# Even mixer of a two-layer trunk: attention steps in pairs, four modulation panels multiplied by TensorE, the output projection cut in halves

## What is computed

```python
c_act = jax.nn.silu(c)
for l in range(DEPTH):
    mod = (c_act @ ada_w[l] + ada_b[l]).reshape(bsz, 6, 1, D_MODEL)
    sh1, sc1, g1, sh2, sc2, g2 = (mod[:, i] for i in range(6))
    h = rms_norm(x, norm1_g[l]) * (1.0 + sc1) + sh1
    ...
    x = x + g1 * y
    h = rms_norm(x, norm2_g[l]) * (1.0 + sc2) + sh2
    x = x + g2 * grouped_moe(h, router_w, router_b, moe_w_gu[l], moe_w_down[l])

def even_mixer(...):
    u, v, q, k, vd = split_cols(h @ w_in, (SGU_WIDTH, SGU_WIDTH, DIFF_QK, DIFF_QK, DIFF_V))
    a_out = spatial_gating(jax.nn.gelu(u), jax.nn.gelu(v), ln_g, ln_b, w_s, b_s)
    b_out = differential_attention(q, k, vd, lam, subln_g, lam_init)
    return jnp.concatenate([a_out, b_out], axis=-1) @ w_out
```

## Time and profile before

| | us |
|---|---|
| times of three runs | 945.0, 945.79, 954.57 |
| median | 945.79 |
| the profiled execution | 948.7 |
| its span in the trace | 947.0 |
| PE busy | 830.0 (88%) |
| DVE busy | 350.0 (37%) |
| ACT busy | 158.3 (17%) |
| mean granted PE clock | 0.947 |
| read from HBM | 292.18 MB, 310 GB/s over the span |

### The profile page before, as it was taken

The page is one execution under the profiler, slowest core; times in us unless marked ns, Lnnn a source line. Parts: engine busy times, 40 slices in busy tenths (PEclk is TensorE's granted clock), DMA queues, the critical chain, the costliest instruction groups (busy, mean ns, idle before and its releaser), DMA issues.

```text
span 947.0 us, 10346 instructions
## 1 busy us (share of the span) xinstructions
PE 830.0 (88%) x4138; PEld 442.1 (47%) x4138; DVE 350.0 (37%) x845; ACT 158.3 (17%) x386; POOL 23.5 (2%) x65
## 2 busy tenths in 40 slices
PE   5999779889998998866999998999899998998863
PEld 2566554454333332222868887865364333332211
DVE  1186586572111111102888663425274111111102
ACT  2031130132111010001101323322222111010001
POOL 2000000010000000000000000000010000000000
PEclk9999799779999999979999998997979999999989
DMA  9999845599999999999989224240429999999993
GB/s 350 389 339 387 317 176 179 206 371 363 362 410 409 409 409 410 409 409 391 387 295 354 89 90 178 90 178 1 178 94 403 378 407 409 410 409 410 409 410 147
DMA packets 96086, 293.98 MB, mean 310 GB/s; under 512 B 2464, under 2 KB 3104, under 8 KB 96032
## 3 DMA queue, kind: packets, MB, share of 16 engines
q1 hardware_dynamic: 95328, 290.61, 79.9%
q10 hardware_dynamic: 560, 2.10, 0.6%
q0 software_dynamic: 144, 0.52, 0.1%
HBM read 292.18 MB, written 1.05 MB: 310 GB/s over the span
## 4 chain that ended last, share of the span: by engine, by line
PE 47%; issue 26%; SPq 12%; DVE 8%; DMA 3%; ACT 3%; POOL 0%; DVEq 0%; POOLq 0%; ACTq 0%
PE bank L764 15%; SPq L474 12%; PE bank L760 9%; PE bank L986 4%; DMA ring<-w_down_dram 2%; PE bank L1005 2%; DVE gb L1415 2%; PE bank L660 2%; PE bank L822 2%; PE bank L677 1%; PE bank L972 1%; PE bank L633 1%; PE bank L668 1%; PE bank L1020 1%; PE bank L799 1%
## 5 line engine op out<-in xcount | busy, mean ns | idle before, releaser
L986 PE MATMUL bank<-ring,scr 128*64 128x512 f32 (+1 forms) x1088 | 210.5, 624 | 38.4 <-DMA ring<-w_gu_dram 24.8
L764 PE MATMUL bank<-hT,ring 128*128 128x256 f32 x640 | 145.5, 388 | 0.8 <-DVE hT L1477 0.8
L986 PEld LDWEIGHTS bank<-ring,scr 128*64 128x64 f32 (+1 forms) x1088 | 61.2, 131 | 173.4 <-issue 136.6
L764 PEld LDWEIGHTS bank<-hT,ring 128*128 128x128 f32 x640 | 123.8, 195 | 19.3 <-issue 2.0
L1005 PE MATMUL bank<-ring,scr 128*64 128x512 f32 (+1 forms) x544 | 102.2, 597 | 8.9 <-DMA ring<-w_down_dram 8.4
L1903 DVE TENSOR_TENSOR hT<-bank,gb 128x512 f32<-128x512 f32 x28 | 19.4, 692 | 199.8 <-PE bank L1005 199.8
L1415 DVE SCALAR_TENSOR_TENSOR gb<-ring,small,gb 128x512 f32<-128x512 f32 x98 | 73.7, 752 | 3.5
L1005 PEld LDWEIGHTS bank<-ring,scr 128*64 128x64 f32 (+1 forms) x544 | 30.1, 127 | 66.6 <-issue 60.9
L760 PE MATMUL bank<-ring,xh 128*128 128x512 f32 x128 | 58.1, 611 | 1.4 <-ACT xh L1170 1.4
L760 PE MATMUL bank<-ring,hT 128*128 128x512 f32 x128 | 58.2, 611 | 0.7 <-ACT hT L1197 0.6
L1020 PE MATMUL bank<-hT,scr 64*128 64x512 f32 x224 | 55.6, 615 | 1.8 <-DVE hT L1903 1.8
(11 more groups left out here) (238 smaller groups left out, 700.1 us busy)
## 6 DMA issues: line engine op xcount, KB each, us to landing
ring<-w_gu_dram SPq DMA_DIRECT2D x64, 2048.0 KB, 22.3
ring<-w_down_dram SPq DMA_DIRECT2D x32, 2048.0 KB, 23.5
ring<-ada_w_dram SPq DMA_DIRECT2D x24, 2048.0 KB, 14.6
ring<-od_w_in_dram SPq DMA_DIRECT2D x9, 2048.0 KB, 16.0
ring<-ev_w_in_dram SPq DMA_DIRECT2D x5, 2048.0 KB, 19.4
ring<-ev_w_out_dram SPq DMA_DIRECT2D x2, 2048.0 KB, 15.3
ring<-od_w_out_dram SPq DMA_DIRECT2D x2, 2048.0 KB, 8.3
xs<-x_dram ACTq DMA_DIRECT2D x1, 1024.0 KB, 5.8
```

Source lines behind the costliest of these rows:

```text
L764: ins = pe.matmul(banks[h][:, m * 256:(m + 1) * 256], w[:, c, (2 * h + m) * P:(2 * h + m + 1) * P], x_part[:, c, :], start=(c == 0 and m = ...
L986: ins = pe.matmul(b[o:o + r, :].rearrange("p (u f) -> p u f", u=2), h[:, c, r * i:r * i + r], wm, start=(first and c == 0), stop=(last and ...
```

## The change

`ATT_PE` and `ATT_ACT` of layer 0 take the steps in pairs. Panels 8 to 11 are multiplied on PE (`late_rows`), copied out by ACT (`late_row_out`) and summed on PE two at a time (`late_sums`); panels 6, 7, 10 and 11 have their sums in the other pair of buffers. In the load order, ada 8 to 11 stand ahead of the output panels and u moves back by two. ACT, not DVE, empties k and vd. The spatial gating and fill 9 (u's second half) move between attention steps 3 and 4. Fill 10, which multiplies u's half of the output panel 0, comes ahead of the transposes of attention's half. `gate_row2` moves ahead of fill 13.

```diff
 PRE = [[("ada", 0), ("ada", 2), ("in", "v"), ("in", "q"), ("ada", 1), ("ada", 3), ("ada", 4), ("ada", 5), ("in", "k"),
-        ("in", "vd"), ("ada", 6), ("ada", 7), ("in", "u"), ("ada", 8), ("ada", 9), ("out", 0), ("out", 1),
-        ("ada", 10), ("ada", 11)],
+        ("in", "vd"), ("ada", 6), ("ada", 7), ("ada", 8), ("ada", 9), ("in", "u"), ("ada", 10), ("ada", 11),
+        ("out", 0), ("out", 1)],
...
-ATT_PE = ["S0 S1 F T0 S2 A0 T1 S3 A1 F T2 S4 A2 T3 S5 A3 F T4 A4 T5 A5 F".split(),
+ATT_PE = ["S0 S1 F T0 S2 T1 S3 A0 A1 F T2 S4 T3 S5 A2 A3 F T4 T5 A4 A5 F".split(),
...
-ATT_ACT = ["S0 S1 F T0 S2 T1 S3 F T2 S4 T3 S5 F T4 T5 F".split(),
+ATT_ACT = ["S0 S1 F T0 T1 S2 S3 F T2 T3 S4 S5 F T4 F T5 F".split(),
...
+        def acc_of(j):
+            return (acc_even if j // 2 % 2 == 0 else acc_odd)[j % 2]
...
-        DVE_EMPTIES = [{"k", "vd", 0, 1}, {"a", 0, 1}]
+        DVE_EMPTIES = [{0, 1}, {"a", 0, 1}]
...
@@ tensor, even() @@
+                def late_rows(*js):
+                    for j in js:
+                        row_products(bank[j % 2], pre_place(0, ("ada", j)))
+                def late_sums(*js):
+                    take(misc)
+                    pe.wait_ge(late_out, js[-1] - 7)
+                    for j in js:
+                        for m in range(4):
+                            o = 4 * (j % 2) + m
+                            ins = pe.matmul(bank[7][:, o:o + 1], acc_of(j)[:, m * P:(m + 1) * P], thirty_second,
+                                            start=True, stop=True)
+                    give(misc, ins)
...
-                attention(0, 0, [[lambda: (fill(0, 6), fill(0, 7), ada(6), ada(7))],
-                                 [lambda: fill(0, 8)], [lambda: fill(0, 9)]])
-                pe.wait_ge(score_out, 6)
-                pe.wait_ge(vn_ready, 2)
+                attention(0, 0, [[lambda: (ada(6), fill(0, 6), fill(0, 7), ada(7))],
+                                 [lambda: (late_rows(8, 9), fill(0, 8), late_sums(8, 9))],
+                                 [lambda: late_rows(10, 11), spatial, lambda: fill(0, 9)]])
                 for t in range(T):
-                    for g in range(4):
-                        ins = pe.matmul(bank[4 + t][:, g * P:(g + 1) * P], wT[:, g, :], vn[:, t, g * P:(g + 1) * P],
-                                        start=True, stop=True)
-                    ins.then_inc(sgu_mixed, 1)
-                ada(8)
-                for feats, made in ((uu, aout_ready), (vg, bout_ready)):
-                    for t in range(T):
-                        pe.wait_ge(made, t + 1)
-                        transposes([feats[:, t, c * P:(c + 1) * P] for c in range(4)])
-                        if t == 0:
-                            gate_rows(0, 0, (0,) if feats is uu else (1,))
+                    turned(uu, aout_ready, t)
+                late_sums(10, 11)
                 pe.wait_ge(turn_free, turn.n)
                 fill(0, 10)
+                for t in range(T):
+                    turned(vg, bout_ready, t)
+                gate_rows(0, 0)
+                pe.wait_ge(turn_free, turn.n)
                 fill(0, 11)
-                ada(9)
                 fill(0, 12)
-                ada(10)
+                gate_row2(0)
                 fill(0, 13)
-                ada(11)
-                gate_row2(0)
...
@@ scalar, even() @@
+                def values_out():
+                    for h in range(2):
+                        wait_fill(act, 0, 6 + h)
+                        act.activation(vv[:, h, :], fill_bank(6 + h, 0)[:, :], ACT.Copy).then_inc(fill_act[0], 1)
+                def late_row_out(j):
+                    pl = pre_place(0, ("ada", j))
+                    act.wait_ge(panel_done[pl.slot], pl.done)
+                    act.activation(acc_of(j), bank[j % 2][:, :], ACT.Copy).then_inc(late_out, 1)
+                def gelu_table():
+                    act.activation(sm(895, 1), ones[:, 0:1], ACT.Gelu_apprx_tanh)
...
+                attention(0, 0, [[values_out], [lambda: late_row_out(8), lambda: late_row_out(9)],
+                                 [lambda: late_row_out(10), lambda: late_row_out(11), gelu_table],
+                                 [lambda: u_out(0)], [lambda: u_out(1)]])
...
@@ vector, norm(ph) @@
-                if ph == 1:
-                    gate_row2_out()
...
@@ vector @@
+            def late_ada_out(j):
+                misc_in()
+                bias = col[:, C_ADAB:C_ADAB + 96].rearrange("p (l k) -> p l k", l=2)
+                dve.tensor_tensor(mod[:, 0, 4 * j:4 * j + 8], bank[7][:, 0:8], bias[:, 0, 4 * j:4 * j + 8], ALU.add)\
+                   .then_inc(misc_free, 1)
...
@@ vector, even() @@
-                for h in range(2):
-                    wait_fill(dve, 0, 4 + h)
-                    dve.tensor_copy(kT[0][:, 2 * h:2 * h + 2, :], fill_bank(4 + h, 0)[:, :].rearrange("p (c n) -> p c n", c=2))\
-                       .then_inc(fill_dve[0], 1)
+                ada(6)
                 ada_out(0, 4)
                 ada_out(0, 5)
                 dve.wait_ge(dist_done, 2)
                 scores(0, 0, 0, sc, nm_ev[:, 0, :], 0)
                 scores(0, 1, 1, sc, nm_ev[:, 0, :], 0)
                 combine(0, 0)
-                ada(6)
+                combine(1, 1)
+                ada_out(0, 6)
                 ada(7)
-                for h in range(2):
-                    wait_fill(dve, 0, 6 + h)
-                    dve.tensor_copy(vv[:, h, :], fill_bank(6 + h, 0)[:, :]).then_inc(fill_dve[0], 1)
-                ada_out(0, 6)
                 ada_out(0, 7)
-                for j in range(2, 6):
-                    scores(0, j, j, sc, nm_ev[:, 1, :], 0)
-                    combine(j - 1, j - 1)
-                    if j == 3:
-                        sub_norm(0)
-                    if j == 4:
-                        sub_norm_scale(0)
-                        ada(8)
+                scores(0, 2, 2, sc, nm_ev[:, 1, :], 0)
+                scores(0, 3, 3, sc, nm_ev[:, 1, :], 0)
+                sub_norm(0)
+                combine(2, 2)
+                combine(3, 3)
+                late_ada_out(8)
+                scores(0, 4, 4, sc, nm_ev[:, 1, :], 0)
+                scores(0, 5, 5, sc, nm_ev[:, 1, :], 0)
+                combine(4, 4)
                 combine(5, 5)
-                sub_norm(1)
-                ada_out(0, 8)
+                sub_norm_scale(0)
...
-                gates_out(0, (0,))
+                dve.wait_ge(bout_ready, 1)
+                sub_norm(1)
+                late_ada_out(10)
                 sub_norm_scale(1)
-                gates_out(0, (1,))
-                ada(9)
+                gates_out(0)
                 residual(0, 10, 0)
-                ada(10)
                 residual(0, 10, 1)
-                ada_out(0, 9)
-                ada(11)
+                gate_row2_out()
                 residual(0, 10, 2)
-                ada_out(0, 10)
                 residual(0, 10, 3)
-                ada_out(0, 11)
```

More of the change, by code:

```diff
@@ L667, in ada_sum @@
                 for m in range(4):
-                    ins = pe.matmul(bank[7][:, m:m + 1], acc[a][:, m * P:(m + 1) * P], ones[:, 0:1],
+                    ins = pe.matmul(bank[7][:, m:m + 1], acc[:, m * P:(m + 1) * P], ones[:, 0:1],
                                     start=True, stop=True)
@@ L834, in even, with spatial, turned @@
                 base = 0
-                ada = lambda j: ada_sum(acc_even, j % 2, pre_place(0, ("ada", j)))
+                ada = lambda j: ada_sum(acc_of(j), pre_place(0, ("ada", j)))
+                def late_rows(*js):
[10 more added lines that the diff above has]
+                    give(misc, ins)
+                def spatial():
+                    pe.wait_ge(score_out, 6)
+                    pe.wait_ge(vn_ready, 2)
+                    for t in range(T):
+                        for g in range(4):
+                            ins = pe.matmul(bank[4 + t][:, g * P:(g + 1) * P], wT[:, g, :], vn[:, t, g * P:(g + 1) * P],
+                                            start=True, stop=True)
+                        ins.then_inc(sgu_mixed, 1)
+                def turned(feats, made, t):
+                    pe.wait_ge(made, t + 1)
+                    transposes([feats[:, t, c * P:(c + 1) * P] for c in range(4)])
                 fill(0, 0)
@@ L881, in odd @@
                         j = 3 + f if f < 4 else 7
-                        ada_sum(acc_odd, j % 2, pre_place(1, ("ada", j)))
+                        ada_sum(acc_odd[j % 2], pre_place(1, ("ada", j)))
                 pe.wait_ge(*emptied(1, 9))
@@ L909, in conv_rows @@
                     give(misc, ins)
-                ada = lambda j: (lambda: ada_sum(acc_odd, j % 2, pre_place(1, ("ada", j))))
+                ada = lambda j: (lambda: ada_sum(acc_odd[j % 2], pre_place(1, ("ada", j))))
                 attention(1, 0, [[F(10)], [F(11)], [F(12)], [F(13)]])
@@ L1250, in even, with u_out @@
```

(21 more changed lines are left out.)

20 lines of the change are left out of this document (11 added, 9 removed).

## The result

The changed kernel takes 939.86 us (median of 16 runs, 932.27 to 942.4), the kernel before 949.56 in runs beside them (16, 945.0 to 956.55). The ratio is 0.9895, 95% interval 0.9873 to 0.9917. The forecast was 935.8 us against 945.8, a ratio of 0.9894. So the step down is the one predicted, and the absolute figure is 4 us off because the median of the kernel before was itself 3.8 us higher over 16 runs than over the three shown. The profiled execution took 938.6 us, 10.1 less than that of before.

The account below looks back on a forecast made before the run. It took the chain of PE, DVE and ACT before `order` as the bound, with PE setting the mixer. Gains of 6.5 + 5.2 = 11.7 us, less 1.7, left 10.0: 945.8 to 935.8 us, range 933.5 to 938 (chance 0.5).

Parts of the forecast that it names:

- The sum on PE: Mixer of layer 0 from 81.67 us: gapless PE pieces add to 87.5 us, fill 13 ends at 169.2, 6.5 us gained.
- The tail: After fill 13: the transposes start 6.0 us after it and not 11.3, with `gate_row2` done earlier; 5.2 us gained.
- One stretch at the lower clock, 1.7 us, on fill 10: Mixer, after short transposes and one-column matmuls ahead of fill 10: 1.7 us taken off the 11.7 us gain.
- Up to 81.67 nothing moves.: Front of the kernel, until fill 6 starts: the change shifts nothing there, 0 us gained or lost.
- DVE is free at about 78.7 in both: Before fill 6: ada 6's first block fills DVE until the sums of 4 and 5, where DVE was free before too.
- `late_rows`, 1.9 for a panel: New PE work in the mixer: four panels at 1.9 us in a row, 7.6 us; tiling-mode switches priced at 0.
- (c): Mixer: PE's added rows are not hidden, a panel costs 6.9 us; 8.3 us slower, 954 us; chance 0.05.
- The stream ends at about 114: Mixer's weight loads: 19 panels at 5.4 us each, the last landing at about 114 us.
- Nothing waits: Mixer's weight loads in the new order: every panel lands before it is asked for, smallest room 12 us.
- (a): Mixer: two or three more lower-clock stretches of 1.7 us leave 5 to 8 us gained, 938 to 941; chance 0.25.
- (b): Experts' stage: the weight stream takes up the gain, the shorter chain only waits; 943.5 to 947 us; chance 0.07.
- (d): Router and first experts: PE keeps its clock, no slow stretch on fill 10; 12.5 to 15 us gained; chance 0.13.

Follow-up runs that it names:

- load_old: Changed kernel with the old load order: u ahead of ada 8 and 9, output panels ahead of ada 10 and 11; 940.73 us, 0.9898 of the kernel before.
- unpaired: Changed kernel with the attention steps in the old order on PE, ACT and DVE, all else as changed; 946.79 us, 0.9966 of the kernel before.
- row2_last: Changed kernel with `gate_row2` behind fill 13 again and its copy by DVE behind the residuals; 938.61 us, 0.9869 of the kernel before.
- dve_all: Changed kernel with panels 8 to 11 multiplied by DVE in its idle stretches, PE keeping only the sums; 929.6 us, 0.9788 of the kernel before; again 932.42, 0.9825.
- split6: Changed kernel with DVE's panel 6 in two parts around the outs of panels 4 and 5, PE's sum between fills 6 and 7; 938.01 us, ratio 0.9851.
- best2: dve_all with split6 and row2_last, DVE's panels one place later and their sums moved; 929.35 us, 0.9825 of the kernel before.

## Why the prediction was right, point by point

By the profiled executions the transposes of the norm came 10.6 us earlier, where 10.0 was forecast, and four small errors made the 0.6: PE's row starts 0.8 earlier than booked (80.90, not 81.67) and is 0.9 shorter at the upper clock, it has 1.0 more of lower clock (2.7, not 1.7), and the tail is 0.1 longer. The mechanism, a gapless row on PE whose pieces add up, is the one that was forecast; that the figure is so near is partly luck.

- **The sum on PE.** Its first term, the sum of panel 6 ahead of fill 6, starts at 80.90 and fill 13 ends at 170.2: 89.3 us, less 2.7 of lower clock (1.9 on fills 6 and 7, 0.8 on the sum) 86.6, where 87.5 was booked. In load_old, whose row has no piece at the lower clock, it is 86.7 by the rows (80.61 to the end of fill 13 at 167.29). The 0.9 booked too much lies in the four panels of rows (7.1 from start to start, 7.6 booked) and the groups T S T S A A (3.2 each, 3.4 booked). Adding up the pieces by their start-to-start times works where an engine has no gaps. That the pieces would have no gaps was the assumption that carried it, and unpaired shows it is the pairs that make it true (2.83 and 2.44 us of wait without them).
- **The tail.** 6.1 us from fill 13 to the transposes, 6.0 booked. But its reason was half wrong. I credited the 5.2 us to `gate_row2` being gone and the rows at the upper clock; row2_last has `gate_row2` back in the tail and 6.2 us all the same. What made the tail short is that its PE pieces run at the upper clock (L722 1.58, before 2.88; L683 3.64, before 5.17) and that PE comes to them without delay. In the kernel before the sum of panel 11 with the waits about it took the tail's first 3.3 us, from the end of fill 13 at 175.7 to 179.00 (timeline before):

```profile
177.42 1.25 PE L668 MATMUL bank<-ones,gb 128*128 128x1 f32 x8 [1.71 <-DVE mod L1424]
```

With these 3.3 us gone and 2.8 saved by the clock, PE is ahead of the scaled tokens and waits for them, 2.52 us in the kernel after and 1.07 in row2_last. The move costs 1.6 us in front of fill 13 and gives nothing behind it.
- **One stretch at the lower clock, 1.7 us, on fill 10.** One came in the mixer of the profiled execution, but elsewhere and twice as long: 3.5 us from 78 to 86, of which 0.8 lie ahead of the row that the forecast adds up and 2.7 in it. Fill 10 took 7.11. In both executions of dve_all it did fall on fill 10, 8.81. Only the count was right; the rows of one execution before the change could not give the place.
- **"Up to 81.67 nothing moves."** The step that was wrong, though the total hides it. "DVE is free at about 78.7 in both" held for DVE's work but not for its order: the outs of panels 4 and 5 stand behind the whole of panel 6 in its queue, and PE waits 2.45 us. The profiled execution hides this, since its front happened to run 3.2 us earlier (the sum after fill 5 at 74.01, before at 77.21). The 3.2 lie in three pieces: in the kernel before the first transposes (at 11.65) took 3.65 us, the row product behind them 3.12 and fill 0 8.83, in the kernel after 3.34, 1.92 and 7.13.
- **Which part of the front counts.** The 1.5 us of the first two pieces moved DVE as well. The 1.7 of fill 0 did not, and the wait ate it: from the copy behind the second row product (L666 at 20.57, L660 at 22.08 before) to the second sum (77.41, before 78.89) it is 56.8 us in both kernels, and in all eight executions of changed kernels with this order on DVE, whether fill 0 took 7.13 or 8.65. So with a front like that of the kernel before nothing does move, and with fill 0 at the upper clock the kernel before would gain where the changed one waits. Two estimates follow from these rows. With the slow front in both, the second sum stands at 78.9, fill 6 3.6 us later as in load_old, and the transposes 91.95 behind it, at 174.5: 12.5 us gained. With the fast front in both, the kernel before would be 3.2 earlier (its DVE idles 4.74 us before k's copies, so nothing there holds PE): 10.6 - 3.2 = 7.4 gained, and some 3 more if it then lost at the lower clock what the kernel after lost. The 9.7 us between the medians lie between the two; which front is the usual one of the kernel before, one execution of it can't say.
- **`late_rows`, 1.9 for a panel.** 3.64 for two, 1.82 each; rival (c) needed 4.8. L683 begins at 102.14 while L828 is modelled to end at 102.20. The Trainium skill, "TensorEngine Tiling (Array Packing)", Key Properties, has a change of tiling mode drain TensorE; at this grain the trace shows no cost of it. The price was right; the alternative, DVE's idle time, I didn't weigh, and it is worth 7 us.
- **The loads.** "The stream ends at about 114" was wrong: it stands still in 95 to 100 (share 0.18), because the slot that panel 11 waits for is free only when vd's fill is over, and the last three are issued only from 98.3 on. "Nothing waits" was right, and load_old shows that the order doesn't matter.
- **The rivals.** (a), two or three stretches, didn't come in the mixer as such, but the one that came cost as much as two. Its price was loose too: of 11.7 us two stretches of 1.7 leave 8.3 and three 6.6, and its lower end of 5 needs a fourth. (b), the stream takes the gain, is excluded: 10.6 us at the transposes, 10.4 at `order`, 10.1 at the end. (d), beyond the sum, needed the router and the experts at a higher clock: 0.95 in 197 to 250, as before.

## What to carry to other kernels

Where one engine has no gaps the new time is the sum of its pieces; so look for what makes gaps (here a step's scores and combine that alternate on DVE, undone by pairs, about two thirds of the gain), and don't give that engine work that another can do in its idle time: the same four panels cost 7.3 us on PE and nothing on DVE. Before a block of 6 us is put ahead of a short operation in an in-order queue, look who waits for the short one, and look at more than one execution: the wait was 2.45 us in one and 1.01 in another, by how early PE came. Gains of this kind are not to be added up: with one taken (split6), DVE came later and PE earlier to the place where the other (dve_all) had hidden its block.

## What the runs showed of the hardware

The scatter between runs of one kernel goes with the granted clock. The kernel before had 45 runs beside the experiments, from 941.3 to 956.5 us, and their time goes with the mean granted clock (correlation -0.84): the 18 runs at or below 947 us have a mean of 945.0 at clock 0.946, the 14 at or above 953 a mean of 954.5 at 0.937. For the changed kernel (22 runs) it is -0.90, from 931.55 us at 0.964 to 942.73 at 0.947. That is as much as the whole change is worth, so a single pair of runs could have shown 0 or 20 us. The stretches at the lower clock come at different places in executions of the same kernel: fills 6 and 7 took 15.84 in one and 13.98 in the other. The rows bear out that idle time and short pieces go before them. Which of such places is hit isn't open altogether: in the twelve profiled executions the first two stretches exclude each other. Fill 0 took 8.56 to 8.83 us in five (before, row2_last, load_old, dve_all, best2), and in all five the scores' matmuls of steps 0 and 1 took 2.03, the upper clock. It took 7.13 in the other seven, and in all seven those matmuls took 2.67 to 3.76. Why, the rows don't show. In the changed order on DVE the first place is the cheaper one, since the wait for DVE covers what fill 0 loses: fill 6 starts at 81.4 to 81.6 after a slow fill 0 (row2_last, load_old, dve_all) and at 82.4 to 84.0 after a fast one. The Trainium skill, "TensorE: Matmul & The Clock Gate", What's actually happening, says the same in general: the number of slow matmuls varies from run to run of one kernel.
